# RWKV-7 chunks of a hybrid decoder trunk: loop written out, inverse ahead of the head sums, head sums by one product with block ones

## The reference, cut to what matters

```python
kk = hs(k * k_k)                                   # heads of 64
kk = kk / jnp.maximum(jnp.sqrt(jnp.sum(kk * kk, axis=-1, keepdims=True)), 1e-12)
k = k * (1.0 + (a - 1.0) * k_a)
y = wkv7(hs(r), hs(decay), hs(k), hs(v), -kk, kk * hs(a))   # a state of 64x64 per head, token by token
mean = jnp.mean(y, axis=-1, keepdims=True)
var = jnp.mean(jnp.square(y - mean), axis=-1, keepdims=True)
y = ((y - mean) * lax.rsqrt(var + GN_EPS)).reshape(bn, s, rw) * ln_w + ln_b
bonus = jnp.sum(hs(r) * hs(k) * r_k, axis=-1, keepdims=True) * hs(v)
y_a = (y + bonus.reshape(bn, s, rw)) * g
```

## Time and profile before

| | us |
|---|---|
| median of three runs | 3038.29 (3038.13 to 3038.56) |
| the profiled execution | 3043.11 |
| its span, first to last instruction | 3041.4 |
| TensorE busy in the span | 2715.3 (89%) |
| VectorE, ScalarE, GpSimd busy | 1142.1, 984.1, 863.6 |
| RWKV stage (352 to 830 us): TensorE, VectorE, ScalarE, GpSimd busy | 413.2, 276.4, 197.2, 145.5 of 478 |
| mean granted clock, whole span and stage | 0.944, 0.93 |

### The profile page before, as it was taken

How to read it: one execution, slowest core, us unless ns; L and a number is a source line. 1 busy time by engine, 2 the same in 40 slices (tenths; PEclk the granted TensorE clock), 3 DMA queues, 4 the chain that set the end, 5 groups by cost and what they waited for, 6 DMA issues and landing times. The chain is left out here.

```text
span 3041.4 us, 38884 instructions
## 1 busy us (share of the span) xinstructions
PE 2715.3 (89%) x13955; PEld 2255.8 (74%) x13955; DVE 1142.1 (38%) x1399; ACT 984.1 (32%) x1437; POOL 863.6 (28%) x654
## 2 busy tenths in 40 slices
PE   6999389889798999999999865667989999999996
PEld 5887178778686888888888655666868888888885
DVE  4112666566414333023320498852133331133302
ACT  3222544444313332123321543654233331133212
POOL 2222223233232222222222237613223222222220
PEclk8999699999899999999999887888989999999998
DMA  2111000000011111111111200001111111111112
GB/s 83 48 48 35 7 1 1 2 2 1 13 43 30 50 46 50 47 47 52 45 49 41 53 24 1 0 0 45 48 31 47 48 48 49 47 48 48 47 50 65
DMA packets 220687, 109.55 MB, mean 36 GB/s; under 512 B 20141, under 2 KB 219335, under 8 KB 220615
## 3 DMA queue, kind: packets, MB, share of 16 engines
q1 hardware_dynamic: 219968, 108.32, 12.3%
q10 hardware_dynamic: 647, 0.24, 0.0%
HBM read 104.35 MB, written 4.19 MB: 36 GB/s over the span
## 5 line engine op out<-in xcount | busy, mean ns | idle before, releaser
L370 POOL TENSOR_TENSOR w_lo_f<-w_raw_f,w_hi_f 128x512 fp32r<-128x512 f32 (+1 forms) x272 | 371.3, 1365 | 1082.0 <-ACT w_hi_f L364 1082.0
L392 PE MATMUL acc_f<-xn_hi_f,w_hi_f 128*128 128x512 f32 x1408 | 435.8, 391 | 9.7 <-DVE xn_lo_f L286 7.6
L392 PE MATMUL acc_f<-xn_lo_f,w_hi_f 128*128 128x512 f32 x1408 | 434.5, 390 | 0.0
L392 PE MATMUL acc_f<-xn_hi_f,w_lo_f 128*128 128x512 f32 x1408 | 434.4, 390 | 0.0
L364 ACT CAST w_hi_f<-w_raw_f 128x512 fp32r<-128x512 f32 (+1 forms) x272 | 164.5, 605 | 726.2 <-PE acc_f L392 726.2
L392 PEld LDWEIGHTS acc_f<-xn_hi_f,w_hi_f 128*128 128x128 f32 x1408 | 264.6, 188 | 69.7 <-issue 10.7
L392 PEld LDWEIGHTS acc_f<-xn_lo_f,w_hi_f 128*128 128x128 f32 x1408 | 265.1, 188 | 55.4
L392 PEld LDWEIGHTS acc_f<-xn_hi_f,w_lo_f 128*128 128x128 f32 x1408 | 264.8, 188 | 55.2
L1685 DVE SCALAR_TENSOR_TENSOR val_f<-acc_f,prm,val_f 128x1023 f32<-128x1023 f32 x88 | 112.8, 1282 | 359.4 <-ACT val_f L1632 353.0
L392 PE MATMUL acc_f<-h_lo_f,w_hi_f 128*128 128x512 f32 x704 | 216.7, 389 | 0.0
L392 PE MATMUL acc_f<-h_hi_f,w_lo_f 128*128 128x512 f32 x704 | 216.7, 389 | 0.0
(11 more groups left out here) (386 smaller groups left out, 4382.4 us busy)
## 6 DMA issues: line engine op xcount, KB each, us to landing
w_raw_f<-in_f_w_up SPq DMA_DIRECT2D x176, 256.0 KB, 2.9
w_raw_f<-in_f_w_down SPq DMA_DIRECT2D x64, 256.0 KB, 2.7
w_raw_e<-in_e_w_in SPq DMA_DIRECT2D x44, 256.0 KB, 2.9
w_raw_g<-in_o_w_glu SPq DMA_DIRECT2D x32, 256.0 KB, 2.7
w_raw_f<-in_f_w_down SPq DMA_DIRECT2D x32, 192.0 KB, 2.4
x_stage<-in_x SPq DMA_DIRECT2D x8, 512.0 KB, 3.4
w_raw_o<-in_e_w_out SPq DMA_DIRECT2D x16, 256.0 KB, 2.7
w_raw_s<-in_o_w_in SPq DMA_DIRECT2D x16, 256.0 KB, 2.7
```

The costliest lines, as they stand in the source:

```text
L370: pool.tensor_tensor(self.lo[:, par, 0:n, :], self.raw[:, par, 0:n, :], self.hi[:, par, 0:n, :].bitcast(F32), op=ALU.subtract).then_inc(w_ ...
L392: last = nc.tensor.matmul(acc[:, h * HALF:(h + 1) * HALF], w[:, par, j, :], x[:, k + j, h * HALF:(h + 1) * HALF], start=first, stop=final)
```

## The change

1. `all_turns` is a Python loop over the 8 chunks; no hardware loop is left.
2. In a turn level 0 of the inverse comes ahead of the last score products, the head sums and the biases of the next chunk; the turned k and v come behind the second score products.
3. All head sums are one product with `head_ones` (128x128, ones in a head's block), whose result has the sum on every channel; the selectors `head_in` and `head_out` and both widening products are gone. `norms` has 128 partitions instead of 8, floors and roots work on 128x512 (or both norms together), and `kk` and `gn` multiply by `norms` in SBUF instead of by PSUM.
4. Ln is split into `k_ln_act` and `y_ln_act`, which reads PSUM itself with scale and bias, so that `y_floor_dve` is gone. Steps move to other levels.

```diff
         def turn_of_pe(pe, c, s, more, late):
+            scores_pe(pe, c, s, 1)
             turn_pe(pe, c, s, K_TOK)
             turn_pe(pe, c, s, V_TOK)
-            for n in (1, 2, 3):
-                scores_pe(pe, c, s, n)
+            scores_pe(pe, c, s, 2)
             if more:
                 lora_codes_pe(pe, c + 1)
-                k_sum_pe(pe, c + 1)
             level0_pe(pe, c)
-            if late:
-                centre_pe(pe, c - 1)
+            scores_pe(pe, c, s, 3)
             for k in range(1, LEVELS):
                 grow_pe(pe, c, k)
                 if more and k == 1:
                     lora_gate_pe(pe, c + 1)
+                    k_sum_pe(pe, c + 1)
                 if late and k == 2:
+                    centre_pe(pe, c - 1)
+                if late and k == 3:
                     y_sum_pe(pe, c - 1)
-                if late and k == 4:
-                    y_wide_pe(pe, c - 1)
-                if more and k == 5:
-                    k_wide_pe(pe, c + 1)
                 if more and k == 6:
                     bonus_pe(pe, c + 1)
                 close_pe(pe, c, k)
...
                 sigmoids_act(act, c + 1)
             for k in range(LEVELS):
                 level_act(act, c, k)
-                if late and k == 0:
-                    centred_act(act, c - 1)
-                if k == 2:
+                if late and k == 2:
+                    centred_act(act, c - 1, not more)
+                if k == 3:
+                    if more:
+                        k_ln_act(act, c + 1)
+                    if late:
+                        y_ln_act(act, c - 1)
                     if more:
                         gate_act(act, c + 1)
-                        roots_act(act, c + 1, 0, 2 if late else 1)
-                    else:
-                        roots_act(act, c + 1, 1, 1)
-                if more and k == 3:
+                if k == 4:
+                    roots_act(act, c + 1)
+                if more and k == 4:
                     exps_act(act, c + 1, 1 - s, 0)
-                if more and k == 4:
+                if more and k == 5:
                     exps_act(act, c + 1, 1 - s, 1)
...
         def turn_of_dve(dve, c, s, more, late):
-            scores_dve(dve, c)
+            scores_dve(dve, c, 0)
+            scores_dve(dve, c, 1)
+            first_dve(dve, c)
+            scores_dve(dve, c, 2)
+            level0_dve(dve, c)
+            scores_dve(dve, c, 3)
             if more:
                 biased_dve(dve, c + 1)
-                floor_dve(dve, c + 1)
-            level0_dve(dve, c)
             for k in range(1, LEVELS):
                 mask_dve(dve, c, k)
                 if more and k == 1:
                     logsum_dve(dve, c + 1)
-                if k == 2:
-                    if late:
-                        y_floor_dve(dve, c - 1)
-                    if more:
-                        k2_dve(dve, c + 1)
+                if k == 2 and more:
+                    k2_dve(dve, c + 1)
+                    floor_dve(dve, c + 1)
                 if k == 3:
                     mid_state_dve(dve, c, s)
-                if late and k == 4:
+                if late and k == 5:
                     gn_dve(dve, c - 1)
-                if more and k == 5:
+                if more and k == 6:
                     zr_dve(dve, c + 1, 1 - s)
-                if more and k == 6:
                     r_dve(dve, c + 1, 1 - s)
                 close_dve(dve, c, k)
...
-            turn_of(eng, 0, 0, True, False)
-            with eng.Fori(0, NCH // 2 - 1) as n:
-                for k in (1, 2):
-                    turn_of(eng, n * 2 + k, k % 2, True, True)
-            turn_of(eng, NCH - 1, 1, False, True)
+            for c in range(NCH):
+                turn_of(eng, c, c % 2, c < last_chunk, c > 0)
```

The new and changed helpers:

```diff
-        def head_sums(bank, sq):
-            for i in range(RT):
-                last = nc.tensor.matmul(bank[0:HEADS, 0:CH], head_in[:, i, :], sq[:, i, :], start=i == 0, stop=i == RT - 1)
-            return last
+        def head_sums(bank, of):
+            return nc.tensor.matmul(bank[:, :], head_ones[:, :], of, start=True, stop=True)
...
+        def k_ln_act(act, c):
+            wait(act, "k_floor", c)
+            up(nc.scalar.activation(norms[:, 0, :, :], norms[:, 0, :, :], ACT.Ln, scale=SUM_SCALE), "k_ln")
+        def y_ln_act(act, c):
+            wait(act, "y_sum", c)
+            wait(act, "gn", c, back=1)
+            up(nc.scalar.activation(norms[:, 1, :, :], psum4(prep_ps[1]), ACT.Ln, scale=SUM_SCALE / HEAD,
+                                    bias=y_eps[:, 0:1]), "y_ln")
+        def roots_act(act, c):
+            first, end = (0 if c <= last_chunk else 1), (2 if c >= 2 else 1)
+            if first == 0:
+                wait(act, "k_ln", c)
+            if end == 2:
+                wait(act, "y_ln", c, back=2)
+            tile_ = norms[:, first:end, :, :]
+            up(nc.scalar.activation(tile_, tile_, ACT.Exp, scale=-0.5, bias=unscale[:, 0:1]), "roots")
...
         def zr_dve(dve, c, s):
-            wait(dve, "k_wide", c)
-            up(tt(T["kk"], T["kk"], psum4(prep_ps[1]), ALU.mult), "kk")
+            wait(dve, "roots", c)
+            up(tt(T["kk"], T["kk"], norms[:, 0, :, :], ALU.mult), "kk")
```

More of the change, by code:

```diff
@@ L795, in bonus_pe @@
             wait(pe, "g_kept", c)
[L796 to L801, removed]
+            up(head_sums(prep_ps[0], T["rk"]), "bonus_sum")
         def centre_pe(pe, c):
             wait(pe, "y", c)
-            if isinstance(c, int) and c == last_chunk:
-                wait(pe, "gn", c, back=1)
-            elif isinstance(c, int) and c == last_chunk - 1:
+            if c == last_chunk:
+                wait(pe, "y_ln", c, back=1)
+            elif c == last_chunk - 1:
                 wait(pe, "turned_kept", c + 1, 2)
@@ L1125, in floor_dve @@
             wait(dve, "k_sum", c)
[L1126 to L1133, removed]
+            wait(dve, "kk", c, back=1)
+            up(nc.vector.tensor_scalar(norms[:, 0, :, :], psum4(prep_ps[1]), 1e-24, None, ALU.max), "k_floor")
         def zr_dve(dve, c, s):
-            wait(dve, "k_wide", c)
-            up(tt(T["kk"], T["kk"], psum4(prep_ps[1]), ALU.mult), "kk")
+            wait(dve, "roots", c)
+            up(tt(T["kk"], T["kk"], norms[:, 0, :, :], ALU.mult), "kk")
             wait(dve, "kk", c)
@@ L1155, in gn_dve, with scores_dve, first_dve @@
         def gn_dve(dve, c):
-            wait(dve, "y_wide", c)
-            up(tt(y_c[:, :, :], y_c[:, :, :], psum4(prep_ps[1]), ALU.mult), "gn")
-        def scores_dve(dve, c):
+            wait(dve, "roots", c + 2)
+            up(tt(y_c[:, :, :], y_c[:, :, :], norms[:, 1, :, :], ALU.mult), "gn")
+        def scores_dve(dve, c, n):
             mask = causal[:, :, :].rearrange("p a t -> p (a t)").unsqueeze(1).to_broadcast([P, 2, 2 * CH])
-            for n in range(4):
-                wait(dve, "a_ps", c, 2 * n + 2)
-                if n == 0:
-                    wait(dve, "y_ps", c, back=1)
-                    wait(dve, "a_zb", c, 2, back=1)
-                for g in range(2):
-                    dst = (a_b if n < 2 else a_k)[g][:, 2 * (n % 2):2 * (n % 2) + 2, :, :]
-                    up(tt(dst.rearrange("p i a t -> p i (a t)"),
-                          score_banks[n][g].rearrange("p (i a) -> p i a", i=2), mask, ALU.mult), "a_kept")
-                if n == 1:
-                    for g in range(2):
-                        wait(dve, "a_kept", c, 3 + g)
-                        wait(dve, f"res_ps{g}", c, 2, back=1)
-                        up(tt(mx[g][:, :, :], a_b[g][:, :, 0, :],
-                              level_mask[:, 0, :].unsqueeze(1).to_broadcast([P, RT, CH]), ALU.mult), "first")
+            wait(dve, "a_ps", c, 2 * n + 2)
+            if n == 0:
+                wait(dve, "y_ps", c, back=1)
+                wait(dve, "a_zb", c, 2, back=1)
+            for g in range(2):
+                dst = (a_b if n < 2 else a_k)[g][:, 2 * (n % 2):2 * (n % 2) + 2, :, :]
+                up(tt(dst.rearrange("p i a t -> p i (a t)"),
+                      score_banks[n][g].rearrange("p (i a) -> p i a", i=2), mask, ALU.mult), "a_kept")
+        def first_dve(dve, c):
+            for g in range(2):
+                wait(dve, "a_kept", c, 3 + g)
+                wait(dve, f"res_ps{g}", c, 2, back=1)
+                up(tt(mx[g][:, :, :], a_b[g][:, :, 0, :], level_mask[:, 0, :].unsqueeze(1).to_broadcast([P, RT, CH]),
+                      ALU.mult), "first")
         def mask_dve(dve, c, k):
@@ L1410, in _ @@
                 exps_act(act, 0, 0, 1)
[L1411 removed]
+                k_ln_act(act, 0)
+                roots_act(act, 0)
                 turn_act(act, 0, B_TOK)
@@ L1466, in _ @@
                 pe.wait_ge(lora_loaded, 48)
-                pe.wait_ge(r_consts, 3)
+                pe.wait_ge(r_consts, 4)
                 pe.wait_ge(eyes, 4)
-                pe.wait_ge(selectors, 2 + RT + 3)
```

51 lines of the change are left out of this document (12 added, 39 removed).

## The result

The change makes the kernel slower. Its median is 3096.64 us over four runs (3094.41 to 3097.36) against 3038.43 us of the kernel before on the same chip (3038.13 to 3043.99): a ratio of 1.0186 [1.0168, 1.0204], or 58 us. The profiled execution took 3096.12 us with a span of 3094.4, which is 53.0 above that of before. The forecast was 3063 with a range of 3041 to 3074: the sign is right, and the time lies outside the range. Of all runs in this document one was in a slower state of the chip, a run of e9 with 3279.98 us at a granted clock of 0.812; the ratios leave it out.

A forecast was written before the change was run, and what follows sets the result against it. TensorE, busy nearly nine tenths of the span, bounds the kernel. Six chunks: 344.0 plus 16.2 of clock, 360.2 against 332.0 (+28.2); ends -3.4; total +24.8, so the median 3038.3 becomes 3063.1 us, range 3041 to 3074.

The forecast's parts named there:

- 0.9 for each of 18: 16.2: TensorE's low clock behind three holes in each of six chunks: 0.9 us each (bounds 0 and 1.54), 16.2 us together.
- the three holes that were counted: TensorE waits ahead of the first `grow` (3.8 us), the centring product (3.1) and in the refinement (3.3).
- The holes, 10.2 us a chunk: TensorE's idle time in a chunk of the new order: holes of 3.8, 3.1 and 3.3 us.
- the third hole: TensorE idle in the refinement for 3.3 us, as VectorE's level 6 operations wait out GpSimd's.
- The work at full clock, 57.3 - 10.2 = 47.1 a chunk: A chunk at full clock, summed from its stretches: 57.3 us with holes, for 52.63 before.
- The ends, -3.4: Prologue -1.6, tail -1.7, chunk 7 -0.9 and chunk 0 +0.8 us: together -3.4.
- The loop, -8.5: The hardware loop's two jumps back go when written out: 2 x (2.55 + 1.7) = 8.5 us saved.
- The offset of 4.8 between median and profiled execution: The median of the kernel before stood 4.8 us below its profiled execution; this was carried over to the changed kernel.
- VectorE gets through: Rival: VectorE's level 6 operations pass between GpSimd's, the third hole is 0.7 us, total 3042 us; chance 0.20.
- the clock holds: Rival: all three holes come but TensorE's clock never goes to the low level, 3047 us; chance 0.06.
- the first hole is not there: Rival: ScalarE's copy comes before the first `grow` needs it, `grow` starts at 6.45 us, total 3030; chance 0.05.
- the second hole: TensorE idle about 3.1 us ahead of the centring product, on VectorE's `k_floor`; if missing, about level with before.

The follow-up runs named there:

- e9: Kernel before, loop and order kept, with only the head sums made one product of block ones, both widening products gone: 3044.71 us, 1.001.
- e6: Changed kernel with four repairs: floor in level 1, codes waiting for own inputs, GpSimd's b ahead of output, ScalarE's X copy ahead of sigmoids: 2996.33 us, 0.9857.
- e1: Changed kernel with products that nothing reads put into TensorE's four holes, no wait shortened: 3059.71 us, 1.0065 against the kernel before.
- e8: Kernel before with ten products that nothing reads in the 2.77 us hole where TensorE waits for the biases: 3037.99 us, 0.9992.
- e3: Changed kernel with the low-rank codes waiting only for their own two inputs and the gate product for `sig_g`: 3074.49 us, 1.0112 against the kernel before.
- e4: Changed kernel with GpSimd making `b` of the next chunk ahead of the last one's four output operations: 3078.93 us, 1.0121 against the kernel before.
- e7: Kernel before with only its hardware loop replaced by a Python loop over eight chunks: 3033.47 us, 0.9977.
- e5: Changed kernel with ScalarE copying X of level 0 ahead of the two sigmoids: 3061.34 us, 1.0067 against the kernel before.
- e11: Kernel of the four repairs with VectorE's biases of the next chunk ahead of its mask of level 0: 2988.79 us, 0.9832 against the kernel before.

## Why the sign was right and the size wrong

The miss is 3096.6 - 3063.1 = 33.5 us. By the prediction's own terms:

- **The clock, "0.9 for each of 18: 16.2".** This term failed by most. The clock took 32.7 us (table of e6), and e1 gets 32.9 back in the same chunks without touching a wait: 16.5 of the miss. By the table of e1 the three holes that were counted cost 25.3 and not 16.2, and the one that was not counted 7.6. The reason given for 0.9, that a longer hole can swallow part of the slow stretch, does not hold: the longest hole, 3.75 us, cost the clock 1.3 to 2.9 us, 2.3 on average, where 1.54 had been read behind one of 2.77. The loss of 1.54 was measured in a chunk with one such hole and, as e8 shows, measured rightly; with several holes in a chunk it was larger behind some and nothing behind another. Even the prediction's upper bound, 1.54 for each of 18, would have given 3074.6.
- **The holes, 10.2 us a chunk.** Measured 10.83: 3.75 for 3.8, 3.07 for 3.1, 2.20 for 3.3, and 1.81 ahead of the codes, which the prediction had at nothing. In the sum this is 3.8 of the miss; that it is so little is luck, as the third hole was taken 1.1 too long in each chunk, 6.6 in all. The missed wait itself is worth 10.9 us in the six chunks, 7.6 of clock and 1.8 in chunk 0, 20 us together, and e3, which takes it away, is 22.2 faster. It comes from the move itself: behind the second score products the codes stand ahead of ScalarE's table load for `sig_g`. The prediction asked what level 0 and the first `grow` wait for in the new order, and not what the codes wait for. This is the second step that failed.
- **The work at full clock, 57.3 - 10.2 = 47.1 a chunk.** Measured 47.95 (287.7 / 6), so 4.9 of the miss. These are small steps taken from before's lengths that came out longer. In e6 the stretch to the first `grow` takes 438.18 - 431.11 - 0.19 = 6.88 for 6.45, level 1 takes 5.4 for 5.1, what lies behind level 6 some 0.3 more, level 2 0.2 less; levels 3 to 6 are right to 0.02.
- **The ends, -3.4.** Measured -0.4, 3.0 of the miss. The prologue by itself came out as forecast. Timelines of TensorE in the prologue, the kernel before, then after:

```profile
358.17 2.08 PE L769 MATMUL prep_ps<-lora_x,lora_w 64*128 64x128 f32 x16 [39.57 <-DVE neg_eye L1426]
...
379.19 1.09 PE L837 MATMUL prep_ps<-ident,b_t 128*128 128x128 f32 x4 [4.66 <-POOL b_t L1225]
```

```profile
359.65 2.08 PE L768 MATMUL prep_ps<-lora_x,lora_w 64*128 64x128 f32 x16 [39.36 <-ACT sig_g L990]
...
370.36 2.07 PE L779 MATMUL prep_ps<-p_even,head_ones 128*128 128x512 f32 x2 [3.95 <-POOL p_even L1214]
379.18 1.09 PE L820 MATMUL prep_ps<-ident,b_t 128*128 128x128 f32 x4 [6.75 <-POOL b_t L1214]
```

  From the first codes to the transposes it is 19.53 us for 21.02, 1.5 less (1.6 forecast), and in e9, which has only the head sums changed, 19.52. But the stage began 1.48 us later. Nothing shows that the change did that: in the twelve traces the first codes start between 356.98 and 359.65 us, and e4, with the same code as after up to there, has them at 359.03, e3 at 358.32. The rest of the 3.0 is chunk 0, which took 2.2 us more for 0.8, as it has the missed hole too. Chunk 7 and the tail together gave the 2.6 expected.
- **The loop, -8.5.** Right: 9.5 in the trace of e7.
- **The offset of 4.8 between median and profiled execution.** It belonged to one execution of before, not to the kernels: after's median stands 0.5 above its profiled time. That is the last 5.3 of the miss.

Together 16.5 + 3.8 + 4.9 + 3.0 + 5.3 = 33.5.

Of the rivals, "VectorE gets through" is out (1.68 and 1.76 us, e4), "the clock holds" too (0.87 to 0.94), and "the first hole is not there" is what e5 builds, one exchange in ScalarE's queue away. Two of the prediction's signs of being wrong can be answered: the second hole was there, and only one of VectorE's four operations ran at its lone length.

What the change was worth is in e6 and e11. With its waits mended a chunk takes 49.1 and 48.0 us, where before had 52.6 and more, but as it was written the new order put four waits in front of TensorE: the codes on ScalarE's table load, `grow` on a copy behind sigmoids, the centring product on a floor that VectorE makes late, the refinement on GpSimd's place in the queue. None of the four repairs changes any arithmetic; each is an exchange in one queue or one count of a wait.

Open is why the same holes cost the clock different amounts from chunk to chunk (61.6 to 65.6 us in after, 57.6 and 61.8 in e5), and whether the head sums by one product help at all inside e11: the old head sums were not put back there.

## What to carry to other kernels

When an order of work changes, list for every instruction of the bounding engine what it waits for and when that is ready in the new order, the unmoved ones too: the missed hole was on products that had kept their place and lost the score product ahead of them. Where TensorE sets the pace, count a hole as itself and its clock apart. In these runs the holes of 1.8 us and more of a chunk cost 1.2 to 1.9 us of clock each on average, the longest ones most, and single ones nothing, so a discount for a long hole was wrong; taking one hole away left the clock's share between two thirds and all of what it was, and it came back whole only when all four were gone. Filling the holes with products that nothing reads is a quick experiment that separates the two. A step's gain is measured from the step's own start and not from that of the program, as in the prologue here, where 1.5 us gained and 1.48 of a later start looked like nothing.

## What the runs showed of the hardware

- The low clock of TensorE costs by the group of holes. Four holes of 1.8 to 3.8 us in a chunk cost 5.5 us of clock each chunk; without the 3.07 us one it was as much (34.3 us for 32.7 over six chunks), as the 2.20 us one, which had cost nothing in five chunks of six, then cost 1.6 in each. 37 idle products in the holes made the kernel 37 us shorter.
- VectorE and GpSimd took turns instruction by instruction: 1.68, 1.76 and 1.22 us for operations that take 0.69, 0.69 and 0.16 at least, and GpSimd's `y_c<-y_c,p_even` and `p_even<-y_c,p_even` took 1.63 and 1.61 where e4 has them at 1.27 and 1.29. Whichever had begun first held the other: in e4 r began 0.22 us ahead of a GpSimd operation and took 0.69, and that operation 1.61. In e4 the 4-element copy `ends` still took 1.25 us, since a GpSimd operation had begun just before it.
- The jump back of the hardware loop left TensorE idle for 2.53 and 2.61 us in the kernel before, 2.80 and 2.78 in e9, and 2.92 + 1.53 and 3.01 + 1.81 us in e8, with ten more products a chunk in its body. Written out (e7), no chunk starts with such a hole.
